# Half-height matmuls in the expert loop: five of six products per bank as halves of 64 rows

## The reference

```python
def expert_block(args):
    xb, e = args                      # 128 rows of 1024
    h = xb @ w_in[e] + b_in[e]        # w_in[e] is 1024 x 2048
    glu = jnp.minimum(h[:, ::2], SWIGLU_LIMIT)
    lin = jnp.clip(h[:, 1::2], -SWIGLU_LIMIT, SWIGLU_LIMIT)
    act = glu * jax.nn.sigmoid(SWIGLU_ALPHA * glu) * (lin + 1.0)
    return act @ w_out[e] + b_out[e]  # w_out[e] is 1024 x 1024
```

## Time and profile before

| | |
|---|---|
| median of the runs | 1472.73 us |
| the profiled execution | 1473.39 us, its span 1471.7 us |
| TensorE busy | 1441.0 us (98%) |
| weight loads busy | 1183.4 us (80%) |
| VectorE busy | 1277.7 us (87%) |
| ScalarE busy | 1019.0 us (69%) |
| GpSimd busy | 240.9 us (16%) |
| loads from memory | 321 GB/s over the span, 370 GB/s in the expert loop |

### The profile page before, as it was taken

How to read it: one execution, slowest core, us unless ns; L and a number is a source line. 1 busy time by engine, 2 the same in 40 slices (tenths; PEclk the granted TensorE clock), 3 DMA queues, 4 the chain that set the end, 5 groups by cost and what they waited for, 6 DMA issues and landing times.

```text
span 1471.7 us, 21956 instructions
## 1 busy us (share of the span) xinstructions
PE 1441.0 (98%) x6833; PEld 1183.4 (80%) x6833; DVE 1277.7 (87%) x1120; ACT 1019.0 (69%) x876; POOL 240.9 (16%) x232
## 2 busy tenths in 40 slices
PE   7999899999999999999999999999999999999997
PEld 6888578778888888888888888888888888888885
DVE  5465747799999999999999999999999999999998
ACT  5423734667777777777777777777777777777774
POOL 0100302412111111111111111212111111111111
PEclk9999999999999999999999999999999999999999
DMA  9442101899999999999999999999999999999994
GB/s 342 177 182 120 44 0 66 303 345 373 365 371 357 375 363 370 367 364 379 364 376 371 379 368 358 389 369 363 373 372 368 370 367 372 367 375 365 367 358 168
DMA packets 131391, 471.72 MB, mean 321 GB/s; under 512 B 15304, under 2 KB 15596, under 8 KB 131176
## 3 DMA queue, kind: packets, MB, share of 16 engines
q1 hardware_dynamic: 118160, 451.46, 81.7%
q0 software_dynamic: 13024, 19.88, 5.5%
q10 hardware_dynamic: 184, 0.08, 0.0%
HBM read 467.44 MB, written 32.51 MB: 340 GB/s over the span
## 4 chain that ended last, share of the span: by engine, by line
PE 91%; DVE 4%; issue 2%; ACT 2%; DMA 1%; DVEq 0%; ACTq 0%
PE pair L993 24%; PE pair L985 24%; PE pair L987 24%; PE pair L714 3%; PE pair L719 3%; PE pair L715 3%; PE pair L999 2%; PE pair L1011 2%; PE pair L975 2%; DVE split L1815 1%; PE pair L856 1%; PE pair L871 1%; PE pair L858 1%; DMA ring<-in_w_moe_in 1%; ACT split L1325 0%
## 5 line engine op out<-in xcount | busy, mean ns | idle before, releaser
L1815 DVE TENSOR_TENSOR split<-ring,split 128x2048 fp32r<-128x2048 f32 x396 | 891.8, 2288 | 71.4 <-ACT split L1325 71.2
L1325 ACT CAST split<-ring 128x2048 fp32r<-128x2048 f32 x396 | 760.0, 1920 | 193.1 <-PE pair L993 190.7
L985 PE MATMUL pair<-split,operands 128*128 128x512 f32 x1584 | 630.0, 398 | 1.0 <-DVE operands L1821 1.0
L987 PE MATMUL pair<-split,operands 128*128 128x512 f32 x1584 | 618.0, 390 | 0.0
L993 PE MATMUL pair<-split,operands 128*128 128x512 f32 x1584 | 424.8, 390 | 0.9 <-DVE split L1815 0.9
L993 PEld LDWEIGHTS pair<-split,operands 128*128 128x128 f32 x1584 | 297.1, 188 | 65.1 <-DVE split L1815 2.1
L985 PEld LDWEIGHTS pair<-split,operands 128*128 128x128 f32 x1584 | 297.7, 188 | 60.1 <-DVE operands L1821 1.4
L987 PEld LDWEIGHTS pair<-split,operands 128*128 128x128 f32 x1584 | 297.9, 188 | 58.5
L2094 POOL DMA_INDIRECT expert_sums<-work,list_cur x32 | 61.8, 1932 | 455.3 <-PE pair L993 423.8
L2087 POOL DMA_INDIRECT work<-h_rows,token_next x34 | 75.2, 2211 | 183.4 <-DMA token_next<-slot_lists 166.7
L1334 ACT CAST operands<-pair 128x512 fp32r<-128x512 f32 x66 | 38.8, 589 | 68.8 <-PE pair L993 39.9
(11 more groups left out here) (268 smaller groups left out, 1149.4 us busy)
## 6 DMA issues: line engine op xcount, KB each, us to landing
ring<-in_w_moe_in SPq DMA_DIRECT2D x264, 1024.0 KB, 9.1
ring<-in_w_moe_out SPq DMA_DIRECT2D x132, 1024.0 KB, 9.9
ring<-in_w_in SPq DMA_DIRECT2D x12, 1024.0 KB, 10.5
ring<-in_w_o SPq DMA_DIRECT2D x4, 1024.0 KB, 10.3
resid<-in_x SPq DMA_DIRECT2D x4, 512.0 KB, 5.2
expert_sums<-zero_rows SPq DMA_DIRECT2D x4, 512.0 KB, 11.9
h_rows<-work SPq DMA_DIRECT2D x4, 512.0 KB
work<-expert_sums SPq DMA_DIRECT2D x4, 512.0 KB, 5.2
```

The costliest lines, as they stand in the source:

```text
L985: pe.matmul(dst[:, f, :], left_hi[:, k0 + k, :], hi[c.buffer][:, k, cols], start=(start and k == 0), stop=False)
L987: pe.matmul(dst[:, f, :], left_lo[:, k0 + k, :], hi[c.buffer][:, k, cols], start=False, stop=False)
L1325: act.copy(hi[c.buffer], raw[c.slot]).then_inc(hi_made, 1)
L1815: dve.tensor_tensor(lo[c.buffer], raw[c.slot], hi[c.buffer].bitcast(F32), ALU.subtract).then_inc(lo_made, 1)
```

## The change

In `product` five of the six products of each bank are cut into two matmuls of 64 rows. A new helper, `halves`, issues one product for both banks: with `swap` 0 rows 0 to 63 go into bank 0 and rows 64 to 127 into bank 1, with `swap` 1 the other way round. A chunk first does five products one way (high by high and low by high for both k, then high by low for k = 0), then the sixth (high by low, k = 1) as two full matmuls of 128 rows, then waits for a new semaphore that the fifth product raises, and then does the same five products the other way round, so that each bank has got both halves of the rows. Chunks of odd number begin with the way that the even ones end with. The low part of the weights is now asked for after four products of one way, no longer after eight matmuls. The bias products become two matmuls of 64 rows, one for each bank.

```diff
+            def half_rows(r):
+                return slice(r * (P // 2), (r + 1) * (P // 2))
...
             def product(p, j, dst, k0, left_hi, left_lo, start, stop):
                 c = Step(p, j)
+                way = j % 2
+
+                def halves(swap, left, right, k, begin, end=False):
+                    for f in ((0, 1) if swap == 0 else (1, 0)):
+                        rows = half_rows(f ^ swap)
+                        mm = pe.matmul(dst[:, f, :], left[rows, k0 + k, :], right[c.buffer][rows, k, f * 512:(f + 1) * 512],
+                                       start=begin, stop=end)
+                    return mm
+
                 pe.wait_ge(hi_made, c.number + 1)
                 for k in range(2):
-                    for f in range(2):
-                        cols = slice(f * 512, (f + 1) * 512)
-                        pe.matmul(dst[:, f, :], left_hi[:, k0 + k, :], hi[c.buffer][:, k, cols],
-                                  start=(start and k == 0), stop=False)
-                        pe.matmul(dst[:, f, :], left_lo[:, k0 + k, :], hi[c.buffer][:, k, cols],
-                                  start=False, stop=False)
+                    halves(way, left_hi, hi, k, start and k == 0)
+                    halves(way, left_lo, hi, k, False)
                 pe.wait_ge(lo_made, c.number + 1)
+                halves(way, left_hi, lo, 0, False).then_inc(one_way_done, 1)
+                for f in range(2):
+                    pe.matmul(dst[:, f, :], left_hi[:, k0 + 1, :], lo[c.buffer][:, 1, f * 512:(f + 1) * 512],
+                              start=False, stop=False)
+                pe.wait_ge(one_way_done, c.number + 1)
+                halves(1 - way, left_hi, lo, 0, False)
                 for k in range(2):
-                    for f in range(2):
-                        cols = slice(f * 512, (f + 1) * 512)
-                        mm = pe.matmul(dst[:, f, :], left_hi[:, k0 + k, :], lo[c.buffer][:, k, cols],
-                                       start=False, stop=(stop and k == 1))
+                    halves(1 - way, left_hi, hi, k, False)
+                    mm = halves(1 - way, left_lo, hi, k, False, stop and k == 1)
                 mm.then_inc(chunk_used, 1)
 
             def bias_of_half(g):
                 for f in range(2):
-                    pe.matmul(pair[g][:, f, :], pick_bias[:, f, :], b_in_parts[:, g * 512:(g + 1) * 512],
+                    rows = slice(f * 2 * NE, (f + 1) * 2 * NE)
+                    pe.matmul(pair[g][:, f, :], pick_bias[rows, f, :], b_in_parts[rows, g * 512:(g + 1) * 512],
                               start=True, stop=False)
```

More of the change, by code:

```diff
@@ L345, in build @@
         w_out_used = sem("w_out_used")
-        sp_passed = sem("sp_passed")
+        one_way_done = sem("one_way_done")
         eps_set = sem("eps_set")
```

## The result

The changed kernel takes 1685.2 us (median of 4 runs, 1682.62 to 1687.34); before, with one more run, 1475.66 us (1472.57 to 1479.18). The ratio is 1.1418, 95% interval 1.1388 to 1.1447: 14% slower. The profiled execution took 1682.62 us, 209.2 more than the profiled one of before. The forecast was 1670, in a range of 1605 to 1705.

A forecast was written before the change was run, and what follows sets the result against it. TensorE's stream was taken to bound the kernel; height changes of 158.4 and 52.8 us, less 15.0 us for the bias, added 196 us to 1473.4 us, giving 1670 us, range 1605 to 1705.

The forecast's parts named there:

- What bounds: In the loop TensorE's stream sets the time, busy 98% of the span; VectorE, 93.5% busy, is the next limit.
- A pair costs what a full matmul cost: Ten pairs of halves a chunk run side by side at 0.2267 us each, so the products' time doesn't change.
- lower bound: A pair in a chunk at 0.2133 us, 512 columns at 2.4 GHz, which would save 53 us.
- A change of height costs 0.20 us: Two changes in each of 396 chunks, 158.4 us, and two at each of 132 transpose groups, 52.8 us.
- the sum: Whole kernel: 158.4 + 52.8 - 15.0 = +196 us on 1473.4 us, giving 1670 us.
- The other edits: Bias products as pairs: 15.0 us less; the new wait for `one_way_done` and the earlier low part: zero.
- The low part's earlier deadline: At chunks behind a swiglu the margin shrinks from 1.32 to 0.41 us; cost zero, at most 60 us.
- No change was hidden: Rival: height changes are hidden in TensorE's stream, giving 1405 to 1460 us; chance 10%.
- The halves ran side by side: Rival claimed the opposite: float32r halves in the chunks run one after another, 898 us more, about 2580 us; chance 6%.
- TensorE did not wait for the low part: Rival claimed it waits behind the swiglu, 60 us on top, up to 1730 us; chance 4%.
- both bounds of the pair's cost: Pairs in the chunks: 0.2133 us each saves 53 us; 0.005 us a pair more adds 20 us.

The follow-up runs named there:

- never turned kernel: Changed kernel with all six products as pairs of halves, always the same way round, no full matmul in a chunk: 1508.99 us, ratio 1.0223.
- two changes: Kernel before with one product of six as two pairs of halves, between eight full matmuls and two full ones: 1641.02 us, ratio 1.112.
- four changes: Kernel before with one product as two pairs of halves, in the order pair, full matmul, pair, full matmul: 1798.28 us, ratio 1.2175.
- bias halves: Kernel before with the changed bias products alone, 66 pairs of halves between full matmuls: 1488.83 us, ratio 1.008.
- early low part: Kernel before, all matmuls full height, low part of the weights asked for after four matmuls of a chunk instead of eight: 1478.31 us, ratio 1.0013.

## Why the prediction was right, and what was off

**What bounds.** Right: TensorE's stream set the time before and after. The change put 6.25 us on it in each pass and nothing covered that.

**A pair costs what a full matmul cost.** Right. In the never turned kernel 144 pairs replace 144 matmuls and the pass grows by 0.95 us, which the changes at the transposes explain. A stretch of pairs without a change runs at 0.227 us a pair. No saving towards the 0.2133 us that I had as the lower bound showed up. The Trainium skill ("TensorE: Matmul & The Clock Gate", "Back-to-back issue gap") calls its N/2.4 + 2.5 ns, 216 ns here, the gap of an isolated matmul (its section "Wait — 56ns, not 53.3ns?" has the same figure for matmuls back to back), and gives 131 ns for 512 columns in a stream with weight loads, which the prediction passed over. Neither figure was reached in these runs, by full matmuls or by pairs.

**A change of height costs 0.20 us.** The mechanism is what the weight loads' rows show, and the count decides: 2, 10 and 12 pairs a chunk, with 2, 2 and 0 changes inside it, lost 164, 210 and 32 us (medians). By this the rule that changing the tiling mode drains TensorE (the Trainium skill, "TensorEngine Tiling (Array Packing)", "Key Properties") agrees with the runs. In the trace the next load starts 0.32 us after the last half does, which is behind its columns but ahead of its recorded end at 0.38 to 0.39 us (that end is modelled). The size was a little low inside the products, 0.207 to 0.221 us, and a little high at the transposes, 0.15 to 0.175. Per pass I had 24 x 0.20 + 8 x 0.20 - 0.453 = 5.95 us; with the two prices of the runs it is 24 x 0.221 + 8 x 0.175 - 0.453 = 6.25. That equals the measured 6.25 by construction, since both prices were taken from differences of the same periods. The independent prices are those of the runs with two changes, four changes and the bias halves, 0.207 to 0.215 us; with 0.214 the sum is 6.08 us, 0.17 short.

What I left out inside the products is the slower start of the stream. In the kernel before it stands behind each group of transposes, in rows I had looked at only for 706.46 to 706.90:

```profile
706.82 0.48 PE L985 MATMUL pair<-split,operands 128*128 128x512 f32 x1
707.14 0.39 PE L987 MATMUL pair<-split,operands 128*128 128x512 f32 x1
707.37 0.40 PE L985 MATMUL pair<-split,operands 128*128 128x512 f32 x1
707.60 0.39 PE L987 MATMUL pair<-split,operands 128*128 128x512 f32 x1
707.83 0.40 PE L985 MATMUL pair<-split,operands 128*128 128x512 f32 x1
708.06 0.39 PE L987 MATMUL pair<-split,operands 128*128 128x512 f32 x1
708.29 0.39 PE L985 MATMUL pair<-split,operands 128*128 128x512 f32 x1
```

From 707.14 to 708.29 are five steps of 0.230 us, against 0.2267 in the earlier trace rows. In the changed kernel every run of halves is too short to leave this stretch: between 320 and 1600 us the pairs that have no change between them start 0.230 us apart on average (0.228 in the never turned kernel). At the transposes the kernel before had paid it already, which fits their lower price; no run tests this by itself. Why a stream starts slower no run tells.

**Where the 13 us beyond the sum are.** 33 x 0.30 = 10 us are the sizes above. The other 3 us are outside the steady passes. At the start of the loop the profiled execution of the changed kernel had two spells at 1.2 GHz, half of the full clock, that the one of before hadn't. The windows, two after and one before:

```profile
281.00:284.50 3.50, 3.50 (x18) 2.50 (x18) 3.50 (x2) 0.54 (x1) 2.97 (x2) 0.51 0.86 242
301.00:309.00 8.00, 7.72 (x34) 4.15 (x30) 6.34 (x9) 2.12 (x2) 2.47 (x2) 0.57 0.75 258
```

```profile
300.00:310.00 10.00, 10.00 (x50) 8.09 (x49) 9.40 (x7) 6.19 (x6) 3.78 (x4) 1.00 0.94 313
```

The clock missing in these two windows is worth at most 3.5 x 0.49 + 8 x 0.43 = 5.2 us, an estimate from their rows, so it is enough for the 3 us; that it is all of them is likely and not shown.

**The other edits.** In the changed kernel a bias pair starts at 800.98 and the product behind it at 801.21, 0.23 us where two slots of 0.227 stood; it saves that only between halves, as the run with bias halves alone shows. The wait for `one_way_done` cost nothing that shows: the gap behind the full matmuls is 0.37 us "issue", as it is in front of them, where no wait stands. The low part's earlier deadline cost nothing, even with TensorE at its old pace.

**The rivals.** No change was hidden, neither around one pair (the bias) nor around two or five, nor at the transposes between whole chunks of twelve. The halves ran side by side. TensorE did not wait for the low part. The range had room for both bounds of the pair's cost, though its lower end was added up wrongly: pairs at their floor and changes at 0.185 give 1670 - 53 - 16 = 1601 us, not 1605. The measured time lies 15 us above the forecast: the changes inside the products were dearer than 0.20 us, partly by a slower stream behind them that the sum had left out.

## What to carry to other kernels

Count the changes of tile height in TensorE's order, not the matmuls: between 64 and 128 rows, in either direction, each cost 0.15 to 0.22 us here, at the most nearly a whole 512-column matmul (0.227), and transposes and bias products count as well. Two halves of 64 rows side by side took what one full matmul takes, so cutting products that fill all 128 rows had nothing to win here and paid for every boundary. TensorE's busy share does not show such pauses; the gaps of the weight loads with the releaser "issue" do, and an earlier stage of the same kernel that alternates heights gives the price ahead of any run.

## What the runs showed of the hardware that was not expected

- **The granted clock can stay at half while TensorE is 100% busy.** With both halves of each pair in rows 0 to 63, the clock fell to 1.2 GHz at about 284 us, shortly behind two waits of 0.69 us, and stayed there for the rest of the loop (0.50 from 1000 to 4000 us, with 3000 of 3000 us busy). The changed kernel fell to half at 281 us too and had the full clock again by 285. With the same number of halves in both row groups it was 1.00 in the loop (700 to 900 us of the never turned kernel). What else can hold it there was not tried.
- **A stream of matmuls starts slower**, at about 0.230 us instead of 0.2267, after transposes, a change of height or a wait.
- **The start of the expert loop may run at half clock for some microseconds, in some executions.** The kernel with the early low part has the same period of a pass as before, but its profiled execution is 5.9 us longer (1479.3 against 1473.39) and had 0.57 of the clock in a window that had the full clock before:

```profile
299.00:307.00 8.00, 7.49 (x22) 5.51 (x21) 7.09 (x9) 2.24 (x2) 2.27 (x1) 0.57 0.73 234
```

  The clock missing there is worth at most 8 x 0.43 = 3.4 us, so it is not all of the difference. The kernel before varies by as much from one execution to the next. In its 20 executions beside the experiments the time went with the mean granted clock: six with 0.997 took 1474.6 us on average, seven with 0.995 took 1477.0, four with 0.993 or 0.994 took 1478.7. Where in those executions the clock was low is not on record.
- **Waiting for one's own signal is cheaper than two changes of height**, 0.37 us against 0.44.
